# Attention steps on TensorE: transposes, score, product with the values, in place of product, score, transposes

## The reference

```python
# first block, mLSTM in its quadratic form (stage ml), 4 heads of 128
s = einsum(q, k) * exp(d - m)          # gate matrix exp(...) beside the score
h = (s @ v) / max(|s.sum()|, exp(-m))
# first block, latent attention (stage mla), 4 heads, q and k of 128 + 64
pr = softmax(where(causal, q @ k.T, -inf)); out = pr @ v
# second block, differential attention (stage df), 4 heads with two softmaxes each
ad = softmax(s0 + bias) - lam * softmax(s1 + bias); od = ad @ v
# second block, forget-gate attention (stage fx), 8 heads of 64
pf = softmax(where(causal, s + cum_q - cum_k, NEG)); of = pf @ v
```

## Time and profile before

| | us |
|---|---|
| median of 3 runs (1442.76 to 1445.69) | 1444.6 |
| the profiled execution | 1443.84 |
| its span, first to last instruction | 1441.7 |
| TensorE busy in it | 1342.7 (93%) |
| VectorE busy | 789.9 (55%) |
| ScalarE busy | 547.7 (38%) |
| mean granted clock of TensorE | 0.958 |

### The profile page before, as it was taken

The page is one execution under the profiler, slowest core; times in us unless marked ns, Lnnn a source line. Parts: engine busy times, 40 slices in busy tenths (PEclk is TensorE's granted clock), DMA queues, the critical chain, the costliest instruction groups (busy, mean ns, idle before and its releaser), DMA issues.

```text
span 1441.7 us, 17264 instructions
## 1 busy us (share of the span) xinstructions
PE 1342.7 (93%) x6220; PEld 1115.0 (77%) x6220; DVE 789.9 (55%) x1215; ACT 547.7 (38%) x886; POOL 97.4 (7%) x93
## 2 busy tenths in 40 slices
PE   7997788989999999999899998998989999999995
PEld 6877677777888888888687787877768788888884
DVE  5875657437544444332466887577576532255434
ACT  5644535434332233332345553455443322223220
POOL 3000000002000000000003223120020000000001
PEclk9998988899999999999899999999989999999997
DMA  4220110122223233333232211111112232222321
GB/s 170 93 83 15 38 44 30 45 73 73 96 94 101 90 100 102 117 102 102 73 97 94 73 45 59 59 59 45 45 59 88 88 102 100 89 89 100 103 93 67
DMA packets 32742, 115.12 MB, mean 80 GB/s; under 512 B 3740, under 2 KB 3740, under 8 KB 32688
## 3 DMA queue, kind: packets, MB, share of 16 engines
q1 hardware_dynamic: 32112, 112.74, 23.6%
q0 software_dynamic: 576, 1.65, 0.4%
HBM read 112.27 MB, written 2.11 MB: 79 GB/s over the span
## 4 chain that ended last, share of the span: by engine, by line
PE 76%; DVE 17%; ACT 4%; issue 2%; DMA 0%; ACTq 0%; SPq 0%; DVEq 0%
PE bank L683 23%; PE bank L685 23%; PE bank L684 23%; DVE w_lo L1589 3%; DVE tiles L1592 3%; DVE arena L1589 2%; DVE tiles L1589 1%; DVE u_lo L1592 1%; DVE probsT L1589 1%; PE bank L763 1%; PE bank L772 1%; DVE residual L1589 1%; PE bank L839 1%; ACT arena L1154 1%; DVE arena L1592 1%
## 5 line engine op out<-in xcount | busy, mean ns | idle before, releaser
L1589 DVE TENSOR_TENSOR w_lo<-raw_slab,w_hi 128x1024 fp32r<-128x1024 f32 x207 | 262.9, 1270 | 309.7 <-ACT w_hi L1145 308.7
L683 PE MATMUL bank<-u_hi,w_hi 128*128 128x512 f32 x980 | 394.3, 402 | 28.5 <-DVE tiles L1589 7.9
L684 PE MATMUL bank<-u_lo,w_hi 128*128 128x512 f32 x980 | 387.3, 395 | 0.0
L685 PE MATMUL bank<-u_hi,w_lo 128*128 128x512 f32 x980 | 387.2, 395 | 0.0
L1145 ACT ACTIVATE w_hi<-raw_slab 128x1024 fp32r<-128x1024 f32 x207 | 217.8, 1052 | 197.6 <-PE bank L685 193.4
L683 PEld LDWEIGHTS bank<-u_hi,w_hi 128*128 128x128 f32 x980 | 187.5, 191 | 76.2 <-issue 18.9
L683 PE MATMUL bank<-arena,w_hi 128*128 128x512 f32 x560 | 220.7, 394 | 3.7 <-DVE arena L1589 2.8
L684 PE MATMUL bank<-arena,w_hi 128*128 128x512 f32 x560 | 219.2, 391 | 0.0
L685 PE MATMUL bank<-arena,w_lo 128*128 128x512 f32 x560 | 219.1, 391 | 0.0
L685 PEld LDWEIGHTS bank<-u_hi,w_lo 128*128 128x128 f32 x980 | 187.4, 191 | 40.7
L684 PEld LDWEIGHTS bank<-u_lo,w_hi 128*128 128x128 f32 x980 | 187.9, 192 | 37.3
(11 more groups left out here) (205 smaller groups left out, 1401.2 us busy)
## 6 DMA issues: line engine op xcount, KB each, us to landing
raw_slab<-in_stream SPq DMA_DIRECT2D x207, 512.0 KB, 3.3
residual<-in_xT SPq DMA_DIRECT2D x8, 256.0 KB, 7.3
out_hT<-residual SPq DMA_DIRECT2D x8, 256.0 KB, 2.1
tiles<-in_pT POOLq DMA_DIRECT2D x2, 256.0 KB, 2.9
tiles<-bias_rows POOLq DMA_DIRECT2D x1, 512.0 KB, 3.8
tiles<-in_positions POOLq DMA_DIRECT2D x1, 256.0 KB, 3.5
square<-in_square POOLq DMA_DIRECT2D x1, 192.0 KB, 5.8
cols<-in_columns POOLq DMA_DIRECT2D x1, 69.0 KB, 4.1
```

The costliest lines, as they stand in the source:

```text
L683: pe.matmul(o, ws[0], xs[0], start=first, stop=False)
L684: pe.matmul(o, ws[0], xs[1], start=False, stop=False)
L685: return pe.matmul(o, ws[1], xs[0], start=False, stop=last)
L1589: return nc.vector.tensor_tensor(o, a, b, op)
```

## The change

In each step of `attention` on TensorE the three parts change their order. Before: product of units s-6 and s-5, score of unit s, transposes of unit s-3. Now: transposes of unit s-3, score of unit s, product of units s-6 and s-5. The statistic, the spread and the fill stay at the end of the step. Nothing else changes; the lists of the other four engines are the same, and so are all waits and all buffers.

```diff
                 for step in range(units + LAG_TAIL[a]):
+                    v = step - LAG_T
+                    if 0 <= v < units:
+                        i = v % ST
+                        o = claim(("pT", a, v))
+                        pe.wait_ge(sem.probs_ready, UNIT0[a] + v + 1)
+                        src = PROB + prob_slot(a, v)
+                        for j in range(i + 1):
+                            last = pe.transpose(o[:, j * P:(j + 1) * P], tiles[:, src, j * P:(j + 1) * P], ident)
+                        last.then_inc(sem.pT_ready, 1)
+                    if step < units:
+                        score(step, step // ST, step % ST)
                     v = step - LAG_PV
                     if 0 <= v < units and v % 2:
...
                         last.then_inc(sem.ctx_ready, 1)
-                    if step < units:
-                        score(step, step // ST, step % ST)
-                    v = step - LAG_T
...
-                        last.then_inc(sem.pT_ready, 1)
                     if tail and at_head(a, step, LAG_HEAD + 1) is not None:
```

## The result

| | before | after |
|---|---|---|
| median of 4 runs each | 1443.68 us | **1421.99 us** (1419.27 to 1426.07) |
| profiled execution | 1443.84 | 1419.27 |
| its span | 1441.7 | 1417.1 |
| TensorE busy in it, mean granted clock | 1342.7, 0.958 | 1326.3, 0.969 |

The changed kernel takes 0.9854 of the time of before (95% interval 0.9823 to 0.9885), 1.5% less. 1436 us was forecast, with a range of 1428 to 1446: the direction was right, and the gain nearly three times as large as foreseen and outside the range. Two executions on record, one of before (2673.60 us) and one of the variant s0t1p (2665.46), took nearly twice as long as all others and are left out everywhere.

A forecast was written before the change was run, and what follows sets the result against it. TensorE was taken as nearly full, with only its idle time in the four stages and the clock to win or lose. 1443.84 - 4 - 1 - 3 = 1435.8, forecast as 1436 us, range 1428 to 1446.

The forecast's parts named there:

- the clock: TensorE's granted clock: counted at zero, with 5 us either way, as the new order has more and shorter waits.
- Rival (C): In ml the clock stays up since no wait is over 1 us: 5 us more, 1431 us; chance 0.09.
- Rival (D): In ml the clock falls once more and one more stretch runs at half speed: 1441 us; chance 0.06.
- the rule on transposes: Trainium skill: transposes do not count as activity for TensorE's clock as other matmuls do; it moved no term.
- the sign the prediction set itself: The prediction called itself wrong if the clock in ml left 0.87 by more than 0.05.
- Part 1: In ml, waits for `gated` and the context bank lose 8.7 us, new waits cost 4.6: about 4 us saved.
- The price: In ml, new waits: 3.6 us for the normalisation and 1.0 for scores meeting the exponential or gate uncovered.
- Part 2: In mla and fx, 6.0 us of added transpose waits against 5.5 of product waits and 1.5 in fill steps: net -1.0.
- Part 3: In df, the earlier copy lets VectorE go on 1.3 us earlier, shortening the fill's wait: 3 us saved.
- (A): VectorE is the pace of all four stages and only the name of the wait changes: 1442 us; chance 0.14.
- (B): In mla and fx the early transposes hold up the score and the delay feeds itself: 1448 us; chance 0.11.

The follow-up runs named there:

- s0t1p: Changed kernel with ml's score parted: first plane, transposes, second plane, product; 1419.30 to 1424.58 us in three runs, 0.9851 of before.
- after_again: The changed kernel run again unaltered; 1420.83 us, 0.9874 of before.
- after_third: The changed kernel run once more unaltered; 1425.52 us, 0.9859 of before.
- mla_only: Kernel before with the new order in stage mla alone; 1436.74 us, 0.9969 of before.
- stp: Kernel before with the order score, transposes, product in all four stages; 1435.94 us, 0.9956 of before.
- tps: Kernel before with the order transposes, product, score in all four stages; 1423.99 us, 0.9867 of before.
- fill_mm: Kernel before with each of 16 matmuls of ml's first score plane issued twice; 1440.78 us, 0.9990 of before.
- fill_tp: Kernel before with 24 of ml's 40 transposes of probabilities issued a second time; 1446.29 us, 1.0017 of before.

## Why the prediction was wrong

**The step that failed is the clock.** The prediction counted it "at zero, with 5 us either way". It measured about 6, all in one direction. Within one kernel the time follows the mean granted clock from run to run: over 173 runs of 15 kernels, each taken against its own mean, by 0.96 us for 0.001 (r = -0.91). Before has 0.9605 on average (67 runs), after 0.9667 (12 runs): 6.2 x 0.96 = 6.0 of the 19.0 us between their means; 13.0 are left for the order itself, near the 11.9 us of idle time that the traces show. This is a relation between runs, not an experiment, so 6 is an estimate. In the profiled pair, which lay further apart than most, the clocks are 0.011 apart, about 10.5 of 24.6 us by the same rate; the 16.4 us less of busy time are more than that, since part of them came back as waiting outside the stages.

The reason given was wrong, too: "more and shorter waits" was taken as neutral. The falls shown above stood behind waits close together or behind one of 2 us and more. The earlier trace rows and the product's wait of up to 1.6 us were in hand, and a glance at the 4 us ahead of the stretch at half clock would have shown 1.09 us of work. Rival (C), the clock stays up since no wait is over 1 us, named the right direction and had 0.09; its own size, 5, was about right, but its condition did not hold (a wait of 2.00 us is left, and the clock falls behind it), and it was put for ml alone, where mla gained as well. Rival (D) and the rule on transposes behind it pointed the wrong way. By the sign the prediction set itself, a clock in the stretch of ml that leaves 0.87 by more than 0.05, it was wrong in the first profile, with 0.93 in the row below; in the other two profiles of the changed kernel, after_again and after_third, it is 0.89, within the 0.05.

```profile
95.80:173.50 77.70, 67.33 (x371) 57.56 (x371) 50.60 (x147) 41.42 (x69) 1.12 (x2) 0.93 0.14 47
```

**Part 1, ml, -4.** Right in mechanism, too small: -5.7 of idle time. `gated` gave 4.4 (7.6 to 3.2; 5.6 forecast), the longest wait of 2.0 stayed as foreseen, the context bank's 3.1 went. The price was over-counted: the waits for the normalisation rose by 1.3 (0.9 to 2.2), not by 3.6, and those for the exponential by 0.5, not 1.0. Why the price was so low I did not test.

**Part 2, mla and fx, -1.** -2.7 of idle time. The product's waits fell by 6.9 over all stages (5.5 forecast), and the transposes' rose by 4.5 (6.0 forecast): both ends a little kinder. mla_only shows the idle term alone, -0.9, and that the clock adds to it; stp and tps put the gain in fx down to the product's new place.

**Part 3, df, -3.** -3.5. The mechanism holds less well than the size: the fill's wait gave 1.2 where 3 was forecast; 2.0 came from the product's wait for the context bank, which the prediction kept in its end of the range and not in its sum. The early copy did reach VectorE, whose waits for the conversion fell from 4.9 to 1.5 us in df, and ScalarE's for the transposes from 22.0 to 7.9; so what is left of the fill's wait seems to come from VectorE's own list.

**Rivals (A) and (B).** VectorE is not the pace of all stages; in ml it is what seems left after the change, as s0t1p suggests. Nothing came of the slower case: the score's new waits are 0.5 us in all.

With the idle time at 11.9 alone the sum would have been 1432, inside the range; with the clock at 6 as well it is 1426, 2 us below it. So the idle terms, though sized too small, did not break the range; the clock did. The mean of the twelve runs of after is 1422.8, another 3 us lower; 2 of these lie in the start of the sum, since the profiled execution, 1443.84, is 2 us over the mean of before (1441.8).

## What to carry to other kernels

In a loop over units of different age, try first what starts the longest chain through the other engines: here transposes, copy, rest, gating. In this kernel its position decided the time (tps equals the change, stp gives a third of it), and it did so in ml above all. And when TensorE is nearly full, look at the few microseconds ahead of each stretch at the low clock: idle time that stands together can be paid for twice, once as idle and once in the work behind it, so a change that takes such a gap away can be worth more than the gap. Adding work elsewhere brought no time that could be measured here (fill_mm, fill_tp).

## What the runs showed of the hardware that I had not expected

- Useless work in the right place made the kernel faster: 44 transposes more, 0.9958 [0.9943, 0.9974].
- A single wait need not be long. Before the fall at 133.8 us the longest pause was 1.56 us, with 1.09 us of work in 4. Yet not every such gap is followed by a fall: in the profile after TensorE was busy 0.67 us of the two from 131 to 133, the row below, and the clock stayed. What tells the two kinds apart I leave open.

```profile
131.00:133.00 2.00, 0.67 (x5) 0.30 (x2) 0.77 (x4) 1.99 (x5) 0.00 (x0) 1.00 0.00 0
```

- Most of the spread between runs of one kernel on one core goes with the clock: 67 runs of before went from 1435.92 us (clock 0.964) to 1448.15 (0.955), with r = -0.94.
